# A two-layer hybrid decoder step on eight cores: two mixer buffers, a residual ring of six, feed-forward in quarters, gated first loads and DRAM-to-DRAM weight casts

## What is computed

```python
for l in range(2):                       # x: (tokens, 1024)
    z = x @ w_in                         # 2576 columns for four mixers
    A: y_a = B * conv3(C * h)                            # short gated convolution
    B: gated linear attention, 4 heads, state 32 x 64    # recurrence over the tokens
    C: silu(LN(dwconv31(a * sigmoid(g)) + b))            # Conformer convolution
    D: u * (tril(W_s) LN(v) + b), chunks of 128          # gMLP
    x = LN(alpha * x + concat(y_a, y_b, y_c, y_d) @ w_out)
    x = LN(alpha * x + relu(x @ w_ff1)**2 @ w_ff2)       # 4096 hidden
```

## Time and profile before

| what | us |
|---|---|
| median of 3 runs (1909.03 to 2091.15) | 1910.0 |
| the profiled execution | 1902.91 |
| its slowest core (core 7), first to last instruction | 1901.4 |
| the eight cores | 1870.1 to 1901.4 |
| TensorE (PE) busy, share | 1658.7, 87% |
| DVE busy, share | 891.5, 47% |
| ACT busy, share | 604.2, 32% |
| POOL busy, share | 150.4, 8% |

### The profile page before, as it was taken

The page is one execution under the profiler, slowest core; times in us unless marked ns, Lnnn a source line. Parts: engine busy times, 40 slices in busy tenths (PEclk is TensorE's granted clock), DMA queues, the critical chain, the costliest instruction groups (busy, mean ns, idle before and its releaser), DMA issues.

```text
span 1901.4 us, 26361 instructions; the slowest of 8 cores (1870.1 to 1901.4 us)
## 1 busy us (share of the span) xinstructions
PE 1658.7 (87%) x9138; PEld 820.9 (43%) x9138; DVE 891.5 (47%) x1668; ACT 604.2 (32%) x975; POOL 150.4 (8%) x172
## 2 busy tenths in 40 slices
PE   2586999899988998679999698998999799986997
PEld 1233444444444544435454243443444355453553
DVE  3344333753276363754326443276326637465225
ACT  1232324341433421515143141334223152243230
POOL 2011110100010010100001011100000000010000
PEclk9788999999998999889999799999999899997999
DMA  9986899953356345466425999995333643333331
GB/s 209 194 195 147 186 196 219 279 169 135 112 188 200 113 155 146 99 207 180 153 89 124 278 196 228 201 270 216 133 133 123 229 149 127 132 114 109 111 131 78
DMA packets 111218, 316.25 MB, mean 166 GB/s; under 512 B 15664, under 2 KB 74064, under 8 KB 85200
## 3 DMA queue, kind: packets, MB, share of 16 engines
q1 hardware_dynamic: 60368, 261.71, 39.7%
q0 software_dynamic: 50720, 52.86, 20.4%
HBM read 295.05 MB, written 73.07 MB: 194 GB/s over the span
## 4 chain that ended last, share of the span: by engine, by line
PE 73%; DMA 12%; DVE 6%; issue 4%; ACT 3%; POOL 1%; another core or an unknown queue 1%; DVEq 0%; SPq 0%; ACTq 0%; POOLq 0%
PE pst L28 73%; DMA s_xbM<-xb 3%; DVE scr L28 2%; DVE s_acc L28 2%; DMA scr<-xp 2%; DMA s_fr<-w_in 2%; DMA s_fr<-w_ff 1%; DMA s_fr<-w_out 1%; ACT scr L28 1%; ACT s_xbF L28 1%; DVE s_fst L28 1%; POOL scr L28 1%; ACT s_castb L28 1%; DMA s_mr<-wc 1%
## 5 line engine op out<-in xcount | busy, mean ns | idle before, releaser
L28 PE MATMUL pst<-s_fr,s_hbuf 128*128 128x512 bf16 x2176 | 485.1, 381 | 18.4 <-DMA s_fr<-w_ff 8.2
L28 PE MATMUL pst<-s_xbF,s_fr 128*128 128x512 bf16 (+1 forms) x2560 | 483.7, 348 | 2.7 <-ACT s_xbF L28 2.6
L28 PEld LDWEIGHTS pst<-s_xbF,s_fr 128*128 128x128 bf16 x2560 | 228.8, 98 | 242.4 <-issue 8.4
L28 PEld LDWEIGHTS pst<-s_fr,s_hbuf 128*128 128x128 bf16 x2176 | 211.9, 98 | 265.9 <-issue 26.0
L28 PE MATMUL pst<-s_xbM,s_mr 128*128 128x512 bf16 (+2 forms) x1280 | 261.4, 358 | 44.5 <-DMA s_xbM<-xb 29.5
L28 DVE SCALAR_TENSOR_TENSOR s_acc<-s_acc,pst 128x512 f32<-128x512 f32 x204 | 138.9, 684 | 330.9 <-PE pst L28 300.2
L28 ACT ACTIVATE scr<-pst 128x512 f32<-128x512 f32 (+8 forms) x270 | 133.8, 516 | 500.2 <-PE pst L28 467.7
L28 DVE TENSOR_TENSOR s_hbuf<-s_sring 128x512 bf16<-128x512 f32 (+1 forms) x220 | 133.5, 610 | 277.7 <-ACT s_sring L28 277.3
L28 ACT ACTIVATE s_sring<-pst 128x512 f32<-128x512 f32 (+1 forms) x320 | 167.4, 533 | 288.3 <-PE pst L28 264.2
L28 DVE SCALAR_TENSOR_TENSOR s_acc<-s_acc,s_fst,s_lng 128x1024 f32<-128x1024 f32 x136 | 173.3, 1279 | 40.0 <-POOL s_fst L28 25.0
L28 PEld LDWEIGHTS pst<-s_xbM,s_mr 128*128 128x128 bf16 (+1 forms) x1280 | 115.2, 100 | 173.0 <-issue 69.3
(11 more groups left out here) (88 smaller groups left out, 951.3 us busy)
## 6 DMA issues: line engine op xcount, KB each, us to landing
s_fr<-wc SPq DMA_DIRECT2D x108, 1024.0 KB, 5.2
wc<-s_fr SPq DMA_DIRECT2D x39, 1024.0 KB, 9.9
s_fr<-w_ff POOLq DMA_DIRECT2D x32, 1024.0 KB, 21.0
s_mr<-wc SPq DMA_DIRECT2D x24, 1024.0 KB, 10.0
s_lng<-lnv SPq DMA_DIRECT2D x16, 1024.0 KB, 10.1
x<-s_acc SPq DMA_DIRECT2D x17, 512.0 KB, 8.3
s_acc<-x SPq DMA_DIRECT2D x17, 512.0 KB, 11.1
s_acc<-xp SPq DMA_DIRECT2D x16, 512.0 KB, 12.5
```

The source lines that it names most:

```text
L28: return lambda e: getattr(e, name)(*a, **k)
```

## The change

1. Two `xbM` and two `ymix` in turn. The sample tokens ride with block 2 (`SMP`), so that the second buffers need only 512 columns.
2. A ring of six residual tiles over all F phases (`acc_i`), and two `lng`, each loaded once a layer.
3. The feed-forward goes in four quarters of 8 hidden chunks; `hbuf` is half as large, `fring` has three slots. In the first quarter, `w_ff1` works on 256 tokens at a time.
4. In the first block, x is loaded as f32 through SP into `acc` and cast by ACT and DVE. The DMAs of `w_out`, of the first F and of `lng` wait for a gate, the first matmul of C in M(0,0).
5. For layer 2 no slot is loaded with a cast: its 23 tiles are cast from DRAM to DRAM by POOL (`w_next`) in S = 1..3 of layer 1, each gated by the second chunk of one group of `w_ff2`; all slots of layer 2 come from `wc`.
6. Evacuations, relu, square and more may run on ACT or DVE (`either`), as the planner finds one free. The keys of each M lie a tenth of a window earlier (`MSHIFT`). Some costs of the planner are others.
7. Scratch space is smaller and reused more, and the scan of B goes in pieces of 128 columns.

```diff
-    def phase(self, start, length=1.0):
+    def phase(self, win, shift=0.0, length=1.0):
...
-                o.key = base[start] + length * tot[start] * cum / mine
+                o.key = base[win] + tot[win] * (length * cum / mine - shift)
...
+    def either(self, afn, vfn, reads=(), writes=(), n=512, rate=1.1):
+        op = self.act(afn, reads, writes, n)
+        op.alt = ("dve", [vfn], 140.0 + rate * n)
+        return op
...
-        xbM = mk("xbM", 8 * NTX, BF16)
+        xbMs = [mk("xbM%d" % i, 8 * (NTX, 512)[i], BF16) for i in range(2)]
-        ymix = mk("ymix", 8 * NTX, BF16)
-        hbuf = mk("hbuf", 16 * NTX, BF16)
-        acc = [mk("acc%d" % i, 1024, F32) for i in range(5)]
-        fring = [mk("fr%d" % i, 4096, BF16) for i in range(4)]
+        ymixs = [mk("ymix%d" % i, 8 * (NTX, 512)[i], BF16) for i in range(2)]
+        hbuf = mk("hbuf", 8 * NTX, BF16)
+        accr = [mk("acc%d" % i, 1024, F32) for i in range(6)]
+        fring = [mk("fr%d" % i, 4096, BF16) for i in range(3)]
...
-        lng = mk("lng", 2048, F32)
+        lngs = [mk("lng%d" % i, 2048, F32) for i in range(2)]
...
-            if S == 0:
-                P.dma("pool", slot.ap(0, [[n, 8], [1, n]]), src, [], slot.k(), dkey=(kind, i), nbytes=nb * 2)
+            if S == 0 and l == 0:
+                P.dma("pool", slot.ap(0, [[n, 8], [1, n]]), src, [("gate",)] if ti >= 5 else [], slot.k(), dkey=(kind, i), nbytes=nb * 2.4)
...
+        def w_next(ti, gate):
+            src, n = w_src(1, ti)
+            gi = 23 + ti
+            P.dma("pool", DAP(wc_d, gi * 128 * WCOLS, [[WCOLS, 128], [n, 8], [1, n]]), src, [gate], [("wc", gi), ("nxk", ti % 4)],
+                  dkey=("nx", ti % 4), nbytes=128 * 8 * n * 4.8)
...
+        def acc_i(S, l, c):
+            k = l * NSB + S
+            return (4 * k + sum(1 for q in range(k) if q % NSB == SMP) + c) % 6
...
-            has_s = S == NSB - 1
+            has_s = S == SMP
+            last = S == NSB - 1
+            xb_i = mcnt[0] % 2
+            xbM = xbMs[xb_i]
+            ymix = ymixs[xb_i]
...
+                    if S == 0:
+                        s_ = hbuf.sub(1024 * c, 1024)
+                        load_acc(S, l, c)
+                        P.act(I("activation", s_.c(0, 512), acc_of(S, l, c).c(0, 512), AF.Copy), acc_of(S, l, c).k(), s_.k(0, 512), 512)
+                        P.dve(I("tensor_copy", s_.c(512, 512), acc_of(S, l, c).c(512, 512)), acc_of(S, l, c).k(), s_.k(512, 1024), 512)
...
+                    if S == 0 and l == 0 and j == 0:
+                        P.all[-1].writes += (("gate",),)
+                        P.lw[("gate",)] = P.all[-1]
...
+            TH = [(0, 256), (256, 256)] + ([(512, 128)] if has_s else [])
...
-            for half in range(2):
-                for g in range(4):
-                    wf, _ = w_load("F", S, l, 7 + half * 8 + g)
+            for half in range(4):
+                for g in range(2):
+                    wf, _ = w_load("F", S, l, 7 + half * 4 + g)
...
-                        for (t0, n) in TT:
+                        for (t0, n) in (TH if half == 0 else TT):
...
-                        P.pe([mm(pb.c(0, 512), hbuf.c(hc * NTX + c * 128, 128), w2[hc // 8].c((hc % 8) * 512, 512), 512,
-                                 hc == 0, hc == 15) for hc in range(16)],
-                             w2[0].k() + w2[1].k() + [("h", hc, c) for hc in range(16)], pb.k())
+                        P.pe([mm(pb.c(0, 512), hbuf.c(hc * NTX + c * 128, 128), w2.c(hc * 512, 512), 512,
+                                 hc == 0, hc == 7) for hc in range(8)],
+                             w2.k() + [("h", hc, c) for hc in range(8)], pb.k())
+                        if l == 0 and S > 0 and c == 1:
+                            P.all[-1].writes += (("pg", S, half, ch),)
+                            P.lw[("pg", S, half, ch)] = P.all[-1]
+                            nxt = (S - 1) * 8 + half * 2 + ch
+                            if nxt < 23:
+                                w_next(nxt, ("pg", S, half, ch))
...
-                P.phase(i + 1.0)
+                P.phase(i + 1, MSHIFT + MGROW * i)
                 emit_M(*order[i + 1])
```

More of the change, by code:

```diff
@@ L21 @@
 NSB = 4
+SMP = 2
+MSHIFT = 0.1
+MGROW = 0.0
 WCOLS = 4224
@@ L125, in dma @@
         return self.add(q, I("dma_start", out=out, in_=in_, **kw), reads, writes, dkey=(q, dkey), cost=cost,
-                        lat=2000.0, nbytes=nbytes)
+                        lat=3000.0, nbytes=nbytes)
     def set_keys(self):
         tot = {}
-        for start, length, ops in self.span:
-            tot[start] = tot.get(start, 0.0) + sum(o.cost for o in ops if o.eng == "pe")
+        for win, shift, length, ops in self.span:
+            tot[win] = tot.get(win, 0.0) + sum(o.cost for o in ops if o.eng == "pe")
         base, t = {}, 0.0
@@ L184, in schedule @@
             ready[be].remove(o)
+            if o.alt:
+                if o.eng == be:
+                    ready[o.alt[0]].remove(o)
+                else:
+                    ready[o.eng].remove(o)
+                    o.eng, o.fns, o.cost = o.alt
+                    o.tab = None
             cost = o.cost
@@ L417, in build_program @@
         fst = mk("fst", 5 * 24, F32)
-        SCRB = 41 * 1024
+        xinb = [mk("xin%d" % i, 1024, BF16) for i in range(1)]
+        SCRB = 35 * 1024 + 768
         scr_t = st.enter_context(nc.sbuf_tensor("scr", [128, SCRB // 2], BF16))
@@ L649, in emit_M @@
                             tview(ac32, j * NT + t0, n, kind), ALU.mult), pb.k() + kac, kcv(gAb, j, LA, 2, t0, n, kind, 2, 2), n)
-                    if kind == "p" and has_s:
+                    if kind == "p" and last:
                         P.dve(I("tensor_tensor", gst.c(j * 34, 2), pb.c(510, 2), ac32.c(j * NT + 510, 2), ALU.mult),
@@ L655, in emit_M @@
                                 ac32.ap(j * NT + 512 + 6, [[8, 16], [1, 2]]), ALU.mult), pb.k() + kac, gst.k(), 32)
-            if not has_s:
+            if not last:
                 for j in range(2):
@@ L810, in emit_M @@
                     finish(po, c - 1, 2, c // 2)
-            if has_s:
+            if last:
                 for h in range(4):
@@ L1032, in lnload, with ln @@
             def lnload(which):
-                P.dma("sp", lng.c(0, 2048), DAP(lnv_d, (l * 4 + 2 * which) * 1024, [[0, 128], [1, 2048]]), [], lng.k(),
-                      dkey="lng", nbytes=1 << 20)
-            def ln(c, last):
+                if S == 0:
+                    P.dma("sp", lngs[which].c(0, 2048), DAP(lnv_d, (l * 4 + 2 * which) * 1024, [[0, 128], [1, 2048]]), [("gate",)],
+                          lngs[which].k(), dkey=("lng", which), nbytes=1 << 20)
+            def ln(c, which, last):
+                lng = lngs[which]
                 f = fst.sub(c * 24, 24)
```

282 lines of the change are left out of this document (151 added, 131 removed).

## The result

| | before | after |
|---|---|---|
| median of the runs, us | 1909.5 | 1862.6 |
| ratio of after to before | | 0.975, 95% interval 0.972 to 0.978 |
| profiled time; span of its slowest core, us | 1902.9; 1901.4 | 1860.2; 1858.5 |
| idle time of TensorE, us | 242.7 | 202.0 |
| stretches at half clock: length; busy in them, us | 178.9; 100.1 | 151.6; 94.8 |

The kernel is faster by 2.5%; forecast was 1805, 5.5%, and a range of 1740 to 1878 that holds the 1862.6. In some executions the cores of one die ran slower, at a lower granted clock, and all medians and ratios from here on leave these out; the 1909.5 is so the middle of two, 1909.0 and 1910.0.

A forecast was written before the change was run, and what follows sets the result against it. TensorE bound in dense stretches, DMA and single buffers between them: idle 242.7 to 155 us (-88), half clock -18, splits +1, together -105, so 1798 us profiled and, with 7 us on top, 1805; range 1740 to 1878.

The forecast's parts named there:

- the third tile lands 20 to 24 us earlier: Start: w_in's third tile, on which B waits, lands earlier without x's casts ahead; 18 us of idle time taken as gain.
- The changes of block: Between blocks, TensorE's idle time falls from 31.7 to 15, 28.6 to 8 and 27.7 to 14 us; 1.5 rises to 4.
- With two buffers the load stands a block earlier: Changes of block: the next xbM input is fetched earlier, so some 20 us of mixer work fill DVE's LayerNorms.
- ACT can take work from it: Adds into acc put 93 us more on DVE; ACT can relieve it, with no gain in us given.
- I leave 2.5 us for stalls: Layer 1: the DRAM-to-DRAM casts fit in the DMA's free time and slow loads beside them, costing only 2.5 us.
- up to 14 us without a stall: Three weight slots: a load may take up to 14 us before TensorE stalls, against 5.2 us in the slot's cycle.
- The last block: End of layer 2: idle time at the last change falls from 23 to 12 us, the tail's rises from 14 to 17.
- The clock: Whole kernel: the 50 us lost at half clock fall with the idle time to 32, 18 less.
- rival (a): Changes of block are bound by DVE, not buffers; three quarters of 62 us come back: 1861; chance 0.20 together with (d).
- (d): Changes of block: the planner lets M run no earlier; 51 us come back, 10 with the clock: 1866; chance 0.20 with rival (a).
- (c): Layer 1: casts of 21 us each fill the DMA, making the kernel slower than before, 1980 us; chance 0.10.
- the quarters: Feed-forward in four quarters: 16 more ends of w_ff1 where TensorE waits for relu and square, +6 us idle.

The follow-up runs named there:

- e3: Changed kernel with only one mixer input and one output buffer (xbM0, ymix0) used: 1860.7 us, 0.977 of the kernel before.
- e10: Changed kernel with every copy, square and scaling back on the engine it had before, so the planner chooses none: 1880.5 us, 0.987 of the kernel before.
- e4: Changed kernel without the split of w_ff1 into runs of 256 tokens: 1876.5 us, 0.985 of the kernel before.
- e9: Changed kernel with one lng tile, reloaded for each norm, instead of two resident ones: 1876.9 us, 0.984 of the kernel before.
- e15: Kernel before with one edit, the first half of w_ff1 in runs of 256 tokens: 1901.1 us, 0.998 of the kernel before.
- e1: Changed kernel without the 23 DRAM-to-DRAM casts, layer 2 computing with layer 1's weights: 1824.4 us, 0.957 of the kernel before.
- e6: Changed kernel with four tiles for x's chunks instead of one, and one shared lng tile: 1869.0 us, 0.984 of the kernel before.
- e14: Changed kernel with f32 copies in the casts' shape, to unused DRAM through SP's queue, replacing the 23 casts: 1892.8 us, 0.993 of the kernel before.
- e2: Changed kernel with layer 2's weights again cast into slots and stored in its first block: 1861.9 us, 0.977 of the kernel before.
- e5: Changed kernel with both DVE passes of each norm over 512 of 1024 columns: 1831.4 us, 0.965 of the kernel before.

## Why the prediction was right and wrong

**The start: right in kind, 7 us short.** 66.1 us became 54.7, forecast 48. The step "the third tile lands 20 to 24 us earlier" was mis-sized: it lands 12.6 us earlier, near the 10 us that I had worked out from the volume. The reading by tiles assumed that a removed cast moves the third tile by a whole tile's time. The five tiles came 7 to 15 us earlier, as the removed volume says.

**The first F: right.** 24.9 us against 24. Its waits are for `s_fr<-w_ff`, 13.1 us in three.

**The changes of block: right size in layer 2, wrong cause, so that size was luck.** "With two buffers the load stands a block earlier" was the step. e3 takes the buffers away and nothing happens. The idle time of the middle blocks did fall from 27.7 to 12.5 us, and the runs that lose are those that undo other parts: the choice of engine (18 to 23 us, e10), the split (14 to 19, e4), the resident `lng` (14 to 17, e9). The split alone in the kernel before gives 5 (e15), so they can't be read as terms of a sum; that they are links of one chain, DVE's and ACT's work at the change, is my reading. I had read the chain's `DMA s_xbM<-xb` as "a buffer is missing". The row also had its length, 22.5 and 25.6 us for 1 MB, where a weight tile took 5.2: the load was slow, whatever the number of tiles. Where the choice of engine stood in my text, as "ACT can take work from it", it had no price.

**Layer 1: the failed step.** "I leave 2.5 us for stalls." Leaving the casts out takes 26.5 us of idle time from this stage (e1), and the whole kernel gains 34 to 38. The cost of one cast was estimated well: 7.3 us of DMA time against 8.6 measured, and the busy sum fits, DMA shares of 0.70 to 0.79. The error was to take a sum that fits for a cover. The casts take the plain loads beside them from 5.3 to 9.0 us, x's stores from 5.2 to 11.2, x's chunks from 7.5 to 14.5. I asked that question of the weight slots alone, where the answer (up to 14 us without a stall) held: TensorE waits only 3.5 us for `s_fr<-wc` in this window. It waits for other loads, of which x's chunks have a single tile:

```profile
PE pst L31 <- DMA s_xin<-xp: 11.2, 2, 6.3
...
PE pst L31 <- DMA scr<-stc: 6.8, 1, 6.8
...
PE pst L31 <- DMA s_mr<-wc: 6.0, 1, 6.0
...
PE pst L31 <- DMA s_fr<-wc: 3.5, 2, 3.0
```

Without the casts the same window begins with

```profile
PE pst L31 <- ACT s_xbF L31: 6.2, 6, 2.2
PE pst L31 <- DMA s_xin<-xp: 5.4, 1, 5.4
PE pst L31 <- DMA s_mr<-wc: 5.2, 1, 5.2
```

Waits put down to a DMA fall from 31.2 to 13.0 us, 18 of the 26.5 us of idle time; the rest isn't traced to one transfer. That the single tile of x matters was tested (e6 against e9); for the state of the sample and M's tile it was not.

The rule of the Trainium skill, "DMA: Bandwidth & Descriptors", section on queues, rings and completion order, that an engine goes round robin between its queues, gave an estimate of 10.4 us for a load beside a cast; the median is 9.0, so the trace agrees roughly. I weighed it for one ring and should have weighed it for every transfer that TensorE waits for. The 14 us point, too, was borne out by e14: there the weight loads take 14.2 us and TensorE waits 39.4 us for them.

**First block of layer 2: right**, 11.9 us against 7, DMA share 0.48 against 0.4. But e2 shows that the time went to layer 1: the change's one large DMA edit gives nothing that can be measured in total.

**The last block: no gain where 8 us were forecast.** 37.0 before, 38.1 after. Its end has 16.2 us of idle time from 1840 on, forecast 17; its change 17 and the middle 5, forecast 12. e5 takes 9 of the 38.1 us by halving the norms' passes, so DVE's norms bound it in part, as the text said.

**The clock: the rule held, its input was off.** Loss per idle time was 50/243 = 0.21 before and is 47.4/202 = 0.23.

**The rivals.** The result lies at rival (a) and (d), 1861 and 1866, by their number but by neither cause: the changes of block did get shorter in layer 2, and in the program now D of the mixers ends ahead of `w_out`. That the time falls in the stated range is so in part luck. The cause is a weak form of (c). (c) had the casts at 21 us of DMA time each; they have 8.6, and cost anyway.

**By size.** Forecast 105 us, measured 47. In the profiled spans the forecast was 1796 us and the kernel took 1858.5, 62 more: 47 of idle time and 15 of clock. Of the 47, 33 are in layer 1, 9 in the last block, 7 in the start, 5 in the first block of layer 2 and 1 in the first F, less 1.5 in the next two blocks and the 6 set aside for the quarters. The casts are 26.5 of layer 1's 33 (e1).

## What to carry to other kernels

A background transfer that fits in the DMA's idle time is not free: ask for each transfer beside it that has a single tile or is issued late, what becomes of it when it takes twice as long. A wait for a load in the chain says "late", not yet "no buffer": compare its length with what the same volume takes elsewhere before you pay for a second tile, and test the tile by itself, as e3 and e6 do. And price each helper edit (engine choice, split, resident constants) at the change of block, since shares over the whole span hide it.

## What the hardware showed that I had not expected

A cast of 1 MB of bf16 from DRAM to DRAM takes 8.6 us of all DMA engines and 20.8 us to land; it costs this kernel 1.5 to 1.7 us. A plain bf16 copy of the same result takes 5.1 to 5.8 us, lands in 8.2 and costs nothing measurable, in rows of 8 KB or 1 KB. An f32 copy takes 11.5 us, lands in 21.5 and costs 3 us. So two transfers, a cast and a plain copy, whose DMA time differs by half differ by 2.5 times in their time to land, and it goes with the f32 source, not with the queue or the packet size. Whether its volume or the spacing of its rows does it stays open; the casts of `w_in`, whose rows lie 10,304 bytes apart, land no sooner (23.7 us) than those of `w_ff1` and `w_ff2` at 16 and 4 KB (20.8), so a particular spacing isn't seen to matter.
